# MLA attention heads 0 to 14: probability tiles turned by VectorE blocks and DRAM instead of TensorE

## The chip, the cores and the metric

One core of a Trainium2 chip. The metric is the device time of one execution in microseconds (us). Before the change it is 2168.78 us, the median of three runs (2168.34 to 2168.89).

## The reference

The program is two model blocks in one launch, for 512 tokens of width 1024 in float32. The first block is a gated mix of a convolution and a forgetting attention, then a feed-forward network. The second block puts 16 meta tokens in front (528 tokens), runs an RWKV-7 mixer and then an MLA (multi-head latent attention) mixer. The change touches only the MLA mixer, whose attention is this:

```python
for s, e in bounds:                       # blocks of 128 queries
    sc = (einsum('bqhd,bkhd->bhqk', q_nope[:, s:e], k_nope[:, :e])
          + einsum('bqhr,bkr->bhqk', q_rope[:, s:e], k_rope[:, :e])) * scale
    p = softmax(where(mask, sc, neg), axis=-1)
    outs.append(einsum('bhqk,bkhd->bqhd', p, v[:, :e]))
o = concatenate(outs, axis=1).reshape(B, L, D_INNER)
return (o * silu(g)) @ w_out
```

There are 16 heads. Each has 128 + 64 query and key features and 128 value features. A query block t (0 to 3) sees 16 + 128(t+1) keys.

## The kernel before

**Data.** Products in full precision are made from three float32r products (`product`, lines 161 to 163): high times high, low times high, high times low. Weights come from DRAM into one of two `raw` buffers, and POOL splits each into `w_hi` (L149) and `w_lo` (L152). Such a weight unit is either one head's `gate` (1024 columns) or a unit `A` or `B` (1280 columns) that holds what two heads need. `load_mla` issues the loads on SP; a load of unit u waits until unit u-1's count of splits shows that its buffer is free.

**One head.** `head_pe`, `head_act` and `head_dve` write out by hand what TensorE (PE), ScalarE (ACT) and VectorE (DVE) do for head h. On PE, before the change: scores of tiles 0 and 1 (L161 to L163, L2752, L2753); the first fills, which are `v0` and `v1` (the values of two heads) in an even head and `rope` (rotated queries of two heads) in an odd one; the value product of head h-1 (`values`, L2791 and L2793); the turns of tiles 0 and 1; scores of tile 2; in an even head `v2`; half of a gate fill; scores of tile 3; the fills `ka`, `qn`, `kb`, which are the next head's keys and queries; the other half of the gate; the turns of tiles 2 and 3.

**A tile's way.** Scores lie in PSUM banks 0 and 1. DVE adds the causal mask and takes the maximum (`maximum`, L2930, L2934). ACT takes the exponential and its sum (L2896). DVE takes the reciprocal (L2939) and, for tiles 2 and 3, scales the tile (L2944); for tiles 0 and 1 ACT does (L2902). The tile is 128 queries by keys, but the value product needs keys on the partitions: `turn` transposes it on PE in pieces of 128 columns into bank 2 or 3 (L2775), one more piece holding the 16 keys that lie beyond (L2777), and `turned_out` copies the result to `probT` (L2952, and L2951 for the 16 rows). `gated` multiplies the finished head by its gate and rounds it (L2919, L2921); POOL makes the low part (`z_low`, L2986).

**Banks and orders that matter.** `v0` and `v2` share bank 4: `v2` may start only when ACT has copied `v0` out (L2674), and that copy waits for `values` of the head before (`act.wait_ge(oo_mm, 2 * x)`), because it overwrites the buffer that `values` reads. `ka` and `kb` share bank 5: `kb` may start only when DVE has made the low part of `ka` (`low_out`, L2699), which stands behind `normalise(3)` in DVE's order. The first fill of a head needs the unit that POOL splits once `kb` of the head before is done. In POOL's order a head's gate split comes next, then `z_low`. `rope_parts` (L2723, a copy; L2725, a subtraction) stands behind the reciprocals of tiles 0 and 1 in even heads and behind `maximum(3)` in odd ones.

**SP.** Before the change SP issues all unit loads in order, then three rows of the output weights (`load_out_rows`). The load of the third waits until POOL has split the first, which waits for the last gate fill in head 14.

Of the kernel before, what the change touches and what calls it, by code (L numbers as in the profile page):

```python
# [70 lines left out]
def program(nc, io, out):  # L71
    with ExitStack() as base:
# [219 lines left out]
        x_land = [sem(f"x_land{t}") for t in range(QB)]  # L292
# [2142 lines left out]
        prob = xT[:, 5:7, :].rearrange("p a b -> p (a b)")  # L2435
        put = region(64)
# [322 lines left out]

        def turn_bank(t):  # L2760
            return 2 + t % 2

        def spill_cols(h, t):

            at = P * min(t + 1, QB - 1)
            return (turn_bank(t) if t < QB - 1 else value_bank(0) if h < MH - 1 else 2), at

        def turn(pe, h, t):
            pe.wait_ge(sc_norm, 4 * h + t + 1)
            if h or t >= 2:  # L2770
                pe.wait_ge(pt_ev, 4 * h + (0, 0, 1, 2 if h < MH - 1 else 3)[t])
            if h and t == QB - 1:
                pe.wait_ge(zt_ev, h)
            for c in range(t + 1):
                nc.tensor.transpose(ps[:, turn_bank(t), P * c:P * c + P], prob_cols(t, P * c, P), ident[:])  # L2775
            bank, at = spill_cols(h, t)
            nc.tensor.transpose(ps[:, bank, at:at + P], prob_cols(t, P * (t + 1), P), ident[:]).then_inc(pt_mm, 1)  # L2777
# [4 lines left out]
        def values(pe, h):  # L2782

            e, bank = h % 2, value_bank(h)
            pe.wait_ge(pt_ev, 4 * h + 4)
            pe.wait_ge(fill_act, ACT_AFTER[FILL_AT["v2", h // 2]])
            if h:
                pe.wait_ge(zt_ev, h)
            for c in range(QB):
                q = slice(max(P * c - N_META, 0), T1)  # L2790
                nc.tensor.matmul(ps[:, bank, q], v_tok[:, c, e, :], probT[:, c, q], start=(c == 0), stop=False)  # L2791
            q = slice(T1 - N_META, T1)
            nc.tensor.matmul(ps[:, bank, q], v_tok[:, QB, e, :], probT[:, QB, q], start=False, stop=True).then_inc(oo_mm, 1)  # L2793
# [31 lines left out]
        def head_pe(pe, h):  # L2825
# [12 lines left out]
            if h:  # L2838
                values(pe, h - 1)
            turn(pe, h, 0)  # L2840
            turn(pe, h, 1)
            scores(pe, h, 2)
            between(1)
# [9 lines left out]
            turn(pe, h, 2)  # L2853
            turn(pe, h, 3)
# [32 lines left out]
        def head_act(act, h):  # L2887
            slots = items_of(h)
            for t in range(QB):
                act.wait_ge(sc_max, 4 * h + t + 1)  # L2890
                if h or t >= 2:
                    act.wait_ge(pt_mm, 4 * h + max(t - 1, 0))
# [32 lines left out]
        def head_dve(dve, h):  # L2925
# [20 lines left out]
            def turned_out(t):  # L2946
                dve.wait_ge(pt_mm, 4 * h + t + 1)
                if h:
                    dve.wait_ge(oo_mm, h)
                bank, at = spill_cols(h, t)  # L2950
                nc.vector.tensor_copy(probT[0:N_META, t + 1, P * t + P - 32:P * t + P], ps[0:N_META, bank, at + P - 32:at + P])  # L2951
                nc.vector.tensor_copy(probT[:, 0:t + 1, P * t:P * t + P],  # L2952
                                      ps[:, turn_bank(t), 0:P * (t + 1)].rearrange("p (a b) -> p a b", b=P)).then_inc(pt_ev, 1)
            turns = h % 2 == 1 and h < MH - 1
# [6 lines left out]
            if h:  # L2961
                gated(dve, h - 1)
            turned_out(0)
            turned_out(1)
# [3 lines left out]
            normalise(2)  # L2968
            if h == MH - 2:
# [4 lines left out]
            normalise(3)  # L2974
            if h + 1 < MH:
# [4 lines left out]
            turned_out(2)  # L2980
            turned_out(3)
# [7 lines left out]
        with nc.Block() as block:  # L2989
            @block.sync  # L2990
            def _(sp):
# [21 lines left out]
                for unit in MLA_UNITS:  # L3013
                    load_mla(sp, unit)
                for k in range(2):
                    load_out_rows(sp, k)
                load_out_rows(sp, 2)
# [344 lines left out]
```

## Time and profile before

| what | us |
|---|---|
| median of three runs | 2168.78 |
| the profiled execution | 2170.27 |
| its span, first to last instruction | 2168.5 |
| the stretch of the 16 heads, first score matmul to last value matmul | about 1765 to 2083 |

The 16 heads take some 318 us of the span. One head takes about 20 us. The profile is of one execution; its times are microseconds from the span's start. A matmul's start is exact and its end modelled, so the distance between the starts of two matmuls is what the first one costs PE.

### The profile page before, as it was taken

How to read it: one execution, taken by the hardware profiler on the slowest of the kernel's cores; microseconds unless marked ns; L12 is line 12 of the kernel's file. 1: busy time of each engine (PE TensorE's matmuls, PEld its weight loads, DVE VectorE, ACT ScalarE, POOL GpSimd, SP SyncE). 2: the span in 40 equal slices, each digit the busy share in tenths (PEclk: the TensorE clock that was granted, in tenths of full speed). 3: DMA queues.
4: the chain of work that ended last, by engine and by line, in shares of the span. 5: the costliest groups of instructions: out<-in, count | busy, mean ns of one | idle time of the engine just before them, and what ended most of it. 6: DMA issues, size and time to landing. Idle time of an engine off the chain costs nothing.

```text
span 2168.5 us, 50089 instructions
## 1 busy us (share of the span) xinstructions
PE 2141.5 (99%) x20795; PEld 1715.8 (79%) x20795; DVE 1284.7 (59%) x2558; ACT 836.7 (39%) x1726; POOL 1175.3 (54%) x829
## 2 busy tenths in 40 slices
PE   8999999999999999999999999999999999999999
PEld 6888887788888767777777777777779788888877
DVE  5465467877850666666666666666652476656621
ACT  4122212333320354555555555555432444444410
POOL 5555566688766264544555544544566453443455
PEclk9999999999999999999999999999999999999999
DMA  4322323333332143333333333333534322222132
GB/s 131 88 78 78 88 88 91 94 97 97 97 110 96 42 126 87 83 82 83 82 92 83 88 87 91 88 90 92 145 79 126 107 78 54 67 56 54 54 129 95
DMA packets 368490, 193.77 MB, mean 89 GB/s; under 512 B 124411, under 2 KB 348793, under 8 KB 367881
## 3 DMA queue, kind: packets, MB, share of 16 engines
q1 hardware_dynamic: 368074, 190.50, 31.8%
q8 instruction: 166, 2.72, 0.5%
q14 instruction: 59, 0.48, 0.1%
q10 hardware_dynamic: 191, 0.07, 0.0%
HBM read 159.18 MB, written 18.52 MB: 82 GB/s over the span
## 4 chain that ended last, share of the span: by engine, by line
PE 93%; DVE 3%; POOL 1%; ACT 1%; issue 1%; DMA 0%; SPq 0%; DVEq 0%; POOLq 0%; ACTq 0%
PE ps L1452 21%; PE ps L161 16%; PE ps L162 15%; PE ps L163 15%; PE ps L1691 4%; PE ps L1707 3%; PE ps L1566 2%; PE ps L1737 2%; PE ps L1680 2%; PE ps L2791 2%; PE ps L1606 1%; PE ps L1651 1%; PE ps L1599 1%; PE ps L1638 1%; PE ps L2775 1%
## 5 line engine op out<-in xcount | busy, mean ns | idle before, releaser
L152 POOL TENSOR_TENSOR w_lo<-raw,w_hi 128x1024 fp32r<-128x1024 f32 (+1 forms) x163 | 416.1, 2553 | 13.6
L149 POOL TENSOR_SCALAR w_hi<-raw 128x1024 fp32r<-128x1024 f32 (+1 forms) x163 | 182.3, 1118 | 399.6 <-PE ps L163 383.2
L161 PE MATMUL ps<-h_hi,w_hi 128*128 128x512 f32 x616 | 242.9, 394 | 2.9 <-DVE h_lo L1129 1.7
L162 PE MATMUL ps<-h_lo,w_hi 128*128 128x512 f32 x616 | 240.8, 391 | 0.0
L163 PE MATMUL ps<-h_hi,w_lo 128*128 128x512 f32 x616 | 240.7, 391 | 0.0
L1452 PE MATMUL ps<-mixed_k,raw 128*64 128x264 f32 x1024 | 146.6, 387 | 0.0
L1452 PE MATMUL ps<-mixed_r,raw 128*64 128x264 f32 x1024 | 144.0, 387 | 0.2 <-ACT ws_b L1771 0.2
L161 PEld LDWEIGHTS ps<-h_hi,w_hi 128*128 128x128 f32 x616 | 116.1, 188 | 28.7 <-DVE h_lo L1129 2.6
L1452 PE MATMUL ps<-mixed_g,raw 128*64 128x264 f32 x1024 | 137.6, 387 | 0.0
L163 PEld LDWEIGHTS ps<-h_hi,w_lo 128*128 128x128 f32 x616 | 116.1, 189 | 24.4
L162 PEld LDWEIGHTS ps<-h_lo,w_hi 128*128 128x128 f32 x616 | 116.2, 189 | 23.1
L1144 DVE SCALAR_TENSOR_TENSOR up_c<-up_raw,params,up_c 128x512 f32<-128x512 f32 x88 | 114.5, 1304 | 22.6 <-ACT up_c L862 21.1
L1452 PE MATMUL ps<-mixed_v,raw 128*64 128x264 f32 x1024 | 125.4, 388 | 0.0
L2083 DVE TENSOR_TENSOR x_m<-ps,lv_pad 128x640 f32<-128x640 f32 (+2 forms) x160 | 110.9, 726 | 16.4 <-PE ps L1691 11.8
L1691 PEld LDWEIGHTS ps<-t_m,mb 128*64 128x64 f32 x2752 | 96.7, 138 | 15.4 <-DVE t_m L2089 0.4
L1691 PE MATMUL ps<-t_m,mb 128*64 128x64 f32 x2752 | 96.9, 222 | 0.2 <-DVE t_m L2089 0.2
L1452 PEld LDWEIGHTS ps<-mixed_v,raw 128*64 128x64 f32 x1024 | 71.2, 137 | 31.3
L2896 ACT ACTIVATE xT<-ps,nmax 128x144 f32<-128x144 f32 (+1 forms) x64 | 34.6, 541 | 135.6 <-DVE nmax L2934 135.3
L1707 PEld LDWEIGHTS ps<-x_m,t_t 128*64 128x64 f32 x2240 | 77.1, 138 | 10.5 <-DVE x_m L2083 0.6
L2026 DVE COPY uv<-ps 64x64 f32<-64x64 f32 x160 | 34.8, 217 | 85.3 <-PE ps L1638 84.8
L2032 DVE TENSOR_SCALAR uv<-ps,ec_c 64x64 f32<-64x64 f32 x144 | 39.9, 277 | 68.2 <-PE ps L1651 67.7
L855 ACT ACTIVATE up_raw<-ps 128x512 f32<-128x512 f32 x40 | 24.0, 599 | 145.3 <-PE ps L163 145.3
(499 smaller groups left out, 5793.4 us busy)
## 6 DMA issues: line engine op xcount, KB each, us to landing
raw<-in_rwkv_w_in_dram SPq DMA_DIRECT2D x64, 512.0 KB, 4.4
raw<-in_w_up_dram SPq DMA_DIRECT2D x44, 512.0 KB, 3.9
raw<-in_w_in_dram SPq DMA_DIRECT2D x41, 512.0 KB, 3.9
raw<-in_w_down_dram SPq DMA_DIRECT2D x22, 512.0 KB, 3.5
raw<-in_mla_w_in_dram SPq DMA_DIRECT2D x22, 512.0 KB, 4.0
sb_kept<-xT SPq DMA_DIRECT2D x16, 528.0 KB, 2.6
xT<-sb_kept SPq DMA_DIRECT2D x16, 528.0 KB, 3.8
raw<-in_mla_w_out_dram SPq DMA_DIRECT2D x16, 512.0 KB, 3.6
```

What stands on the lines that cost most here:

```text
L149: nc.gpsimd.tensor_scalar(w_hi[s][:, 0:width], raw[s][:, 0:width], 1.0, 0.0, ALU.mult, ALU.add).then_inc(split_hi, 1)
L152: nc.gpsimd.tensor_tensor(w_lo[s][:, 0:width], raw[s][:, 0:width], w_hi[s][:, 0:width].bitcast(F32), ALU.subtract).then_inc(split_ready, 1)
L161: nc.tensor.matmul(dst, w[0], x[0], start=start, stop=False)
L162: nc.tensor.matmul(dst, w[0], x[1], start=False, stop=False)
L163: return nc.tensor.matmul(dst, w[1], x[0], start=False, stop=stop)
L1144: nc.vector.scalar_tensor_tensor(out=up_c[:, ab, 1 + k, :], in0=up_raw[:, n % 4, 1 - k:1 - k + T1], scalar=prm(("cf1", "cf0")[k], n // 2 + ...
L1452: mm = nc.tensor.matmul(dst[m, :], raw_k[t % 2][:, k, m], mixed[t][:, k, cols], start=(k == 0), stop=(k == KD - 1))
L1566: mm = nc.tensor.matmul(ps[r, banks[h], 0:T2 // 2], WHOLE_W[n][:, P * b + r.start:P * b + r.stop], z_whole[:, k, at:at + T2 // 2], start=s ...
L1680: mm = nc.tensor.matmul(ps[:, 2 + 3 * h + q, x * P:x * P + P], bk[own[h], c0 + x, :], rkv[own[h], c0 + x, 0:2 * C], start=True, stop=True)
L1691: mm = nc.tensor.matmul(ps[own[h], 2 + p, x * C:x * C + C], mb[:, c0 + x, own[h]], t_m[:, c0 + x, :], start=True, stop=True)
L1707: mm = nc.tensor.matmul(dst, t_t[:, c0 + x, :], x_m[:, c0 + x, h, :], start=True, stop=True)
L2083: nc.vector.tensor_tensor(x_m[:, c0:c0 + m, :, :], part_of(2 + p, m).unsqueeze(2).to_broadcast([P, m, 2, C]), lv_pad[:, lv - 1, :, :].unsq ...
```

## The change

In heads 0 to 14 PE turns nothing. DVE transposes each tile in blocks of 32 by 32 (`blocked`), in SBUF; that leaves each block turned in its own place. SP then writes the tile to DRAM with four DMAs, one for each 32 partitions (`write_blocks`), whose runs of 32 elements land so that the DRAM tensor holds the tile with keys as rows, and reads it back into `probT` with one DMA (`read_turned`). The piece with the 16 last keys is turned by a second small DVE transpose and copied (`spilled`). Head 15 keeps the turns on PE. `values` of a head stands one place later in the next head, behind the scores of tile 2. `gated` stands behind `blocked(2)` instead of ahead of `maximum(2)`. The loads of weights are interleaved with the DMAs of the heads: six units ahead of them, then one behind the writes of tiles 0 and 1 and one behind the last reads of each head. Two DRAM scratch tensors per tile alternate from head to head. The core of the diff:

```diff
@@ -2433,6 +2433,11 @@
         assert put.end <= 121
         probT, z_t = xT[:, 0:5, 0:T1], xT[:, 7, 0:T1]
         prob = xT[:, 5:7, :].rearrange("p a b -> p (a b)")
+        p_last = region(154)("p_last", [P, T1 + 32])
+        p_scr = [[nc.dram_tensor(f"p_scr{t}_{e}", [P * (t + 1), P], F32, kind="Internal").ap() for t in range(QB)] for e in range(2)]
+        p_blocked, p_written, p_here = x_land[0:3]
+        LANDED0 = 16
+        BLOCKED, WRITTEN, HERE = 4, 256, 64
         put = region(64)
         o_tok = put("o_tok", [P, QB, D])
         squares = put("squares", [P, QB, D])
@@ -2757,19 +2762,64 @@
             slot = T2 * (1 - t % 2)
             return prob[:, slot + at:slot + at + n]
 
+        def blocks_of(t):
+
+            return (wa_in[:, 0:P], wa_in[:, P:3 * P], wa_in[:, 0:3 * P], p_last[:, 0:T1])[t]
+
+        def spill_of(t):
+
+            return wa_in[0:32, 3 * P + 32 * t:3 * P + 32 * t + 32]
+
+        def write_blocks(sp, h, t):
+            sp.wait_ge(p_blocked, LANDED0 + BLOCKED * h + t + 1)
+            if t == 0 and h > 1:
+                ge(sp, p_here, LANDED0 + HERE * (h - 1))
+            for a in range(4):
+                sp.dma_start(p_scr[h % 2][t].rearrange("(b i) q -> i b q", i=32)[:, :, 32 * a:32 * a + 32],
+                             blocks_of(t)[32 * a:32 * a + 32, :].rearrange("i (b j) -> i b j", j=32)).then_inc(p_written, 16)
+
+        def read_turned(sp, h, t):
+            q = slice(P * t, P * t + P)
+            sp.dma_start(probT[:, 0:t + 1, q], p_scr[h % 2][t].rearrange("(c p) q -> p c q", p=P)).then_inc(p_here, 16)
+
+        def turned_by_dma(sp, h, loads):
+
+            written = LANDED0 + WRITTEN * h
+            write_blocks(sp, h, 0)
+            write_blocks(sp, h, 1)
+            next(loads, None)
+            sp.wait_ge(p_written, written + 128)
+            ge(sp, oo_mm, h)
+            read_turned(sp, h, 0)
+            read_turned(sp, h, 1)
+            write_blocks(sp, h, 2)
+            write_blocks(sp, h, 3)
+            sp.wait_ge(p_written, written + WRITTEN)
+            read_turned(sp, h, 3)
+            read_turned(sp, h, 2)
+            next(loads, None)
+
+        def unit_loads(sp):
+            for unit in MLA_UNITS:
+                load_mla(sp, unit)
+                yield
+            for k in range(3):
+                load_out_rows(sp, k)
+                yield
+
         def turn_bank(t):
             return 2 + t % 2
 
         def spill_cols(h, t):
 
             at = P * min(t + 1, QB - 1)
-            return (turn_bank(t) if t < QB - 1 else value_bank(0) if h < MH - 1 else 2), at
+            return (turn_bank(t) if t < QB - 1 else 2), at
 
         def turn(pe, h, t):
             pe.wait_ge(sc_norm, 4 * h + t + 1)
-            if h or t >= 2:
-                pe.wait_ge(pt_ev, 4 * h + (0, 0, 1, 2 if h < MH - 1 else 3)[t])
-            if h and t == QB - 1:
+            if t >= 2:
+                pe.wait_ge(pt_ev, 4 * h + (1, 3)[t - 2])
+            if t == QB - 1:
                 pe.wait_ge(zt_ev, h)
             for c in range(t + 1):
                 nc.tensor.transpose(ps[:, turn_bank(t), P * c:P * c + P], prob_cols(t, P * c, P), ident[:])
@@ -2782,6 +2832,8 @@
         def values(pe, h):
 
             e, bank = h % 2, value_bank(h)
+            if h < MH - 1:
+                pe.wait_ge(p_here, LANDED0 + HERE * (h + 1))
             pe.wait_ge(pt_ev, 4 * h + 4)
             pe.wait_ge(fill_act, ACT_AFTER[FILL_AT["v2", h // 2]])
             if h:
@@ -2835,11 +2887,13 @@
             scores(pe, h, 1)
             between(0)
             first_out(pe, h, 0)
-            if h:
+            if h == MH - 1:
                 values(pe, h - 1)
-            turn(pe, h, 0)
-            turn(pe, h, 1)
+                turn(pe, h, 0)
+                turn(pe, h, 1)
             scores(pe, h, 2)
+            if 0 < h < MH - 1:
+                values(pe, h - 1)
             between(1)
             if h == MH - 2:
                 fill(pe, FILL_AT["gate", MH - 1], range(5, KD))
@@ -2850,8 +2904,9 @@
             if h + AHEAD < MH:
                 fill(pe, FILL_AT["gate", h + AHEAD], range(2, 5) if h == MH - 3 else range(4, KD))
             first_out(pe, h, 3)
-            turn(pe, h, 2)
-            turn(pe, h, 3)
+            if h == MH - 1:
+                turn(pe, h, 2)
+                turn(pe, h, 3)
 
         def out_pe(pe):
 
@@ -2888,8 +2943,10 @@
             slots = items_of(h)
             for t in range(QB):
                 act.wait_ge(sc_max, 4 * h + t + 1)
-                if h or t >= 2:
-                    act.wait_ge(pt_mm, 4 * h + max(t - 1, 0))
+                if h == MH - 1 and t >= 2:
+                    act.wait_ge(pt_mm, t - 1)
+                elif h or t >= 2:
+                    act.wait_ge(p_blocked, LANDED0 + BLOCKED * h + max(t - 1, 0))
                 dst = prob_cols(t, 0, keys(t))
                 if t == QB - 1:
                     dst = dst.rearrange("p (a b) -> p a b", a=2)
@@ -2944,41 +3001,67 @@
                 nc.vector.tensor_scalar(p, p, prec[:, t % 2:t % 2 + 1], None, ALU.mult).then_inc(sc_norm, 1)
 
             def turned_out(t):
-                dve.wait_ge(pt_mm, 4 * h + t + 1)
-                if h:
-                    dve.wait_ge(oo_mm, h)
+                dve.wait_ge(pt_mm, t + 1)
+                dve.wait_ge(oo_mm, h)
                 bank, at = spill_cols(h, t)
                 nc.vector.tensor_copy(probT[0:N_META, t + 1, P * t + P - 32:P * t + P], ps[0:N_META, bank, at + P - 32:at + P])
                 nc.vector.tensor_copy(probT[:, 0:t + 1, P * t:P * t + P],
                                       ps[:, turn_bank(t), 0:P * (t + 1)].rearrange("p (a b) -> p a b", b=P)).then_inc(pt_ev, 1)
-            turns = h % 2 == 1 and h < MH - 1
+
+            def blocked(t):
+                dve.wait_ge(sc_norm, 4 * h + t + 1)
+                if t == 0:
+                    ge(dve, p_written, LANDED0 + WRITTEN * h)
+                    ge(dve, pt_ev, 4 * h)
+                elif t == 2:
+                    dve.wait_ge(p_written, LANDED0 + WRITTEN * h + 128)
+                nc.vector.transpose(blocks_of(t), prob_cols(t, 0, P * (t + 1)))
+                slot = T2 * (1 - t % 2) + P * (t + 1)
+                nc.vector.transpose(spill_of(t), prob[96:P, slot:slot + 32]).then_inc(p_blocked, 1)
+
+            def spilled(t):
+                dve.wait_ge(p_blocked, LANDED0 + BLOCKED * h + t + 1)
+                ge(dve, oo_mm, h)
+                nc.vector.tensor_copy(probT[0:N_META, t + 1, P * t + P - 32:P * t + P], spill_of(t)[0:N_META, :]).then_inc(pt_ev, 1)
+            last = h == MH - 1
+            turns = h % 2 == 1 and not last
             maximum(0)
             maximum(1)
             normalise(0)
             normalise(1)
             if not turns and h < MH - 1:
                 rope_parts(dve, h + 1)
-            if h:
+            if last:
                 gated(dve, h - 1)
-            turned_out(0)
-            turned_out(1)
+            for t in range(2):
+                turned_out(t) if last else blocked(t)
             maximum(2)
             if turns:
                 rope_turned(dve, h // 2 + 1)
             normalise(2)
+            if not last:
+                blocked(2)
+                if h:
+                    gated(dve, h - 1)
+                for t in range(3):
+                    spilled(t)
             if h == MH - 2:
                 gate_out(dve, MH - 1)
             maximum(3)
             if turns:
                 rope_parts(dve, h + 1)
             normalise(3)
+            if not last:
+                blocked(3)
+                spilled(3)
             if h + 1 < MH:
                 for kind in ("ka", "qn", "kb"):
                     low_out(dve, (kind, h + 1))
             if h + AHEAD < MH - 1:
                 gate_out(dve, h + AHEAD)
-            turned_out(2)
-            turned_out(3)
+            if last:
+                turned_out(2)
+                turned_out(3)
 
         def z_low(pool, h):
             pool.wait_ge(zt_ev, h + 1)
@@ -3010,11 +3093,13 @@
                 sp.dma_start(h_rows_kept, h_rows[:]).then_inc(s_h, 16)
                 for n in range(4, 7):
                     load_in(sp, n)
-                for unit in MLA_UNITS:
-                    load_mla(sp, unit)
-                for k in range(2):
-                    load_out_rows(sp, k)
-                load_out_rows(sp, 2)
+                loads = unit_loads(sp)
+                for _ in itertools.islice(loads, 6):
+                    pass
+                for h in range(MH - 1):
+                    turned_by_dma(sp, h, loads)
+                for _ in loads:
+                    pass
                 sp.wait_ge(unit_done, UNIT_AT["gate", MH - 1] + 1)
                 sp.wait_ge(s_h, 48)
                 sp.dma_start(h_fin[:], h_rows_kept).then_inc(s_h, 16)
```

## Rows read from the trace of the kernel before

**Rows 1.** Windows, the heads: length, busy time of engines, clock, DMA share, GB/s.

```profile
1785.00:2046.00 261.00, 259.99 (x1505) 221.18 (x1505) 158.42 (x407) 125.25 (x254) 113.96 (x65) 1.00 0.23 60
```

**Rows 2.** Timeline of PE, heads 6 and 7: start, duration, what.

```profile
1884.85 0.31 PE L161 MATMUL ps<-kn_hi,qn_hi 128*128 128x144 f32 x1
...
1891.32 0.31 PE L2775 MATMUL ps<-ident,xT 128*128 128x128 f32 x1
...
1891.82 0.43 PE L161 MATMUL ps<-kn_hi,qn_hi 128*128 128x400 f32 x1
...
1892.81 0.28 PE L161 MATMUL ps<-w_hi,ckv_hi 128*16 128x256 f32 x1
...
1901.59 0.29 PE L163 MATMUL ps<-ckv_hi,w_lo 128*128 128x264 f32 x1
...
1904.51 0.49 PE L2775 MATMUL ps<-ident,xT 128*128 128x128 f32 x3
...
1905.40 0.31 PE L161 MATMUL ps<-kn_hi,qn_hi 128*128 128x144 f32 x1
...
1906.68 0.40 PE L161 MATMUL ps<-cq_hi,w_hi 128*128 128x512 f32 x1
...
1920.91 0.36 PE L161 MATMUL ps<-ckv_hi,w_hi 128*128 128x264 f32 x1
...
1925.40 0.31 PE L161 MATMUL ps<-kn_hi,qn_hi 128*128 128x144 f32 x1
```

**Rows 3.** Timeline of POOL, around heads 6 and 7.

```profile
1887.28 2.39 POOL L152 TENSOR_TENSOR w_lo<-raw,w_hi 128x1024 fp32r<-128x1024 f32 x1
...
1902.19 1.26 POOL L149 TENSOR_SCALAR w_hi<-raw 128x1280 fp32r<-128x1280 f32 x1 [8.07 <-PE ps L163]
1903.54 2.94 POOL L152 TENSOR_TENSOR w_lo<-raw,w_hi 128x1280 fp32r<-128x1280 f32 x1
```

**Rows 4.** Timeline of ACT, head 6.

```profile
1891.57 1.09 ACT L2674 ACTIVATE v_tok<-ps 128x512 f32<-128x512 f32 x2 [0.94 <-PE ps L2793]
```

**Rows 5.** Timeline of DVE, heads 6 and 7.

```profile
1888.16 1.79 DVE L2723 CAST qr<-q_rot 64x512 fp32r<-64x512 f32 x1
...
1900.22 0.43 DVE L2699 TENSOR_TENSOR kn_lo<-ps,kn_hi 128x264 fp32r<-128x264 f32 x1
...
1911.98 0.69 DVE L2919 TENSOR_TENSOR xT<-ps,gate 128x512 f32<-128x512 f32 x1 [3.30 <-PE ps L2793]
...
1914.92 0.69 DVE L2708 SCALAR_TENSOR_TENSOR q_rot<-ps,cos_t 128x512 f32<-128x512 f32 x1 [0.25 <-ACT q_sw L2660]
...
1917.50 0.30 DVE L2930 TENSOR_TENSOR ps<-ps,causal 128x128 f32<-128x128 f32 x1
...
1920.22 0.43 DVE L2699 TENSOR_TENSOR kn_lo<-ps,kn_hi 128x264 fp32r<-128x264 f32 x1
```

**Rows 6.** Groups of DVE by shape: busy, mean ns of one, idle before.

```profile
L2092 DVE STREAM_TRANSPOSE t_t<-t_m 128x320 f32<-128x320 f32 x64 | 32.7, 512 | 2.2
L2008 DVE STREAM_TRANSPOSE e_both<-bk 128x128 f32<-128x128 f32 x120 | 31.7, 285 | 4.6 <-POOL bk L2151 4.6
```

**Rows 7.** Timeline of SP, one burst of small copies in the RWKV stage.

```profile
1209.35 12.21 SPq L2315 DMA_DIRECT2D bk_rows<-e_both  x16
```

**Rows 8.** One line of the kernel, these copies: count, ns min/median/max, first and last.

```profile
L2315 SPq DMA_DIRECT2D bk_rows<-e_both x240: 595/611/1767, 800.0 to 1527.6; - x120
```

**Rows 9.** DMA, that burst's stretch 1209:1222: packets, MB, share; KB, landing.

```profile
q1 hardware_dynamic: 5195, 1.05, 40.9%
...
bk_rows<-e_both SPq DMA_DIRECT2D x16, 32.0 KB, 2.5
```

**Rows 10.** DMA, the heads 1790:2070: packets, MB, share; KB, landing.

```profile
q1 hardware_dynamic: 32210, 17.80, 22.9%
...
raw<-in_mla_w_q_up_dram SPq DMA_DIRECT2D x12, 256.0 KB, 3.3
```

**Rows 11.** Timeline of SP, heads 14 and 15.

```profile
2048.09 13.95 SPq L136 DMA_DIRECT2D raw<-in_mla_w_out_dram  x2
```

More of the change, by code:

```diff
@@ L290, in program @@
         x_copied = sem("x_copied")
-        x_land = [sem(f"x_land{t}") for t in range(QB)]
+        x_land = [sem(n) for n in ("x_land0_p_blocked", "x_land1_p_written", "x_land2_p_here", "x_land3")]
         low = region(0)
```

## Prediction

> **What bounds the kernel now.** I read four views. First the busy times by stage: over the heads PE is busy 260.0 of 261 us at full clock, DVE 158 us, and the DMA engines 23% [rows 1]. So a head lasts as long as PE's list of work, and PE's work taken away is a gain only if nothing else that PE waits for is as late. Second, PE's timeline of an even and the next odd head: head 6 starts at 1884.85, head 7 at 1905.40, head 8 at 1925.40, so 20.55 and 20.00 us; I write "place" for the time since a head's first score matmul [rows 2]. Third, what stands beside PE on the other engines at the places the change touches [rows 3 to 5]. The reader is to see there that three waits of PE are met with hardly anything to spare:
> - *The split.* POOL ends `w_lo` at 1903.54 + 2.94 = 1906.48, and PE starts `rope`, which needs it, at 1906.68 [rows 2, 3]. Where PE does wait, a start follows a release by about that. Between the end of `kb` (1901.59 + 0.13 = 1901.72) and that start PE has 4.96 us of other work, all of it needed as cover.
> - *The copy of v0.* In even heads ACT copies `v0` out only after the value product (1891.57) [rows 4]; PE has 1.49 us between the end of that product (1891.32) and `v2` (1892.81) [rows 2], in which the copy fits.
> - *The low part of ka.* In an odd head DVE ends it at 1920.65 and PE starts `kb` at 1920.91 [rows 2, 5]; PE's own work would let it start 0.2 us sooner. DVE already decides there. In the even head the same part ends at 1900.65 and `kb` starts at 1900.97: 0.3 us to spare at most.
>
> Fourth, SP and the DMA views, for what the new copies cost [rows 7 to 11].
>
> **What is removed.** Turns of tiles 0 and 1: 1891.32 to 1891.82, 0.50 us. Of tiles 2 and 3: 1904.51 to 1905.40, 0.89 us [rows 2]. 1.4 us a head, 15 heads: 21 us of PE. The DVE copies from PSUM go too.
>
> **What is added, engine by engine.**
>
> *DVE.* A block transpose of 128 columns takes 285 ns, of 320 columns 512 ns [rows 6], 1.2 ns a column, so about 0.44, 0.57 and 0.71 us for 256, 384 and 512. They take the place of PSUM copies of nearly the same cost, and four small transposes come on top (the same line gives 0.17 us at 32 columns). The sum matters little; the order does. Before, `gated` and the copies of tiles 0 and 1 ran from 1911.98 to the mask of tile 2, while DVE had time. Now `blocked(2)` (0.65), `gated` (1.07) and three `spilled` (0.3) stand between `normalise(2)` and `maximum(3)`, and `blocked(3)` and `spilled(3)` (0.9) ahead of the low part of `ka`: 2.9 us more on the chain to `kb`.
>
> Odd head, place by place. The rotation of the queries waits for ACT's copies as before (1914.92 is place 9.5) [rows 5]; with `normalise(2)` it ends at 12.0, `blocked(2)` at 12.7, `gated` at 13.7, `spilled` at 14.0. From the mask of tile 3 to `ka`'s low part takes 1920.22 - 1917.50 = 2.7 us with the rope parts [rows 5], to 16.8; plus 0.9, and 0.43 for itself: 18.2; `kb` at 18.45. PE gets there at 15.7 (15.5 before, less the 0.5 of the turns, plus 0.85 of the next part, less the 0.2 it already waited). Wait 2.7, of which 0.2 was there: +2.5 us.
>
> *POOL.* The turns of tiles 2 and 3 were cover for the split. PE's work there falls from 4.96 to 4.07 and its start does not: +0.85 us in each of 14 heads.
>
> *ACT.* `v2` now follows the value product directly. Release 0.25, copy 0.6, release 0.2: 1.05 us of waiting in each even head from 2 on. (In head 0 the cover shrinks as well; about 1 us.)
>
> *SP and DMA.* No row shows a store to DRAM of runs of 128 bytes. The nearest is the RWKV stage's copy of 32 KB pieces, also runs of 128 bytes: 16 issues in 12.21 us, 0.76 us each [rows 7], 2.5 us from issue to landing [rows 9]. In that stretch a packet took 0.409 x 16 x 13 / 5195 = 16 ns; in the heads, with runs of 512 bytes and 256 bytes, 0.229 x 16 x 280 / 32210 = 32 ns [rows 9, 10]. A head's 5120 small packets over 16 engines are then 5 to 10 us of a head's time on top of 23%: not a bound. The issues are: sixteen stores are 12.2 us of SP, four reads and two units' loads 4.2 us more. I take 0.76 and 2.5 us, as the burst has the same run, partitions and destination stride; the ends are 0.61, an issue's own time [rows 8], and 2.0 below, and 0.76 and 4 above. A read of up to 256 KB lands in 3.3 us [rows 10].
>
> In an odd head the stores of tiles 0 and 1 start at 3.9 and are landed at 11.8, ahead of `blocked(2)`, which waits for them since the buffer is shared. In an even head they start later. `rope_parts` stands ahead of `blocked(0)`, and its copy ended at 1889.95 after 1.79 us, when POOL's `w_lo` had ended at 1889.67 [rows 3, 5]; it takes 0.4 us otherwise. POOL's gate split now ends at place 5.7 (it starts when the wait for the split ends), so `blocked(0)` ends at 7.05, eight issues start by 12.4 and the last is landed at 14.9. `blocked(2)` comes at 15.0 instead of 12.4, and `kb` at 21.2 where PE is ready at 17.5: a wait of 3.7 us.
>
> The Trainium skill has a rule for that copy (SBUF — State Buffer, Who interferes with whom): a copy in VectorE's two-port mode and a GpSimd instruction exclude each other for the whole instruction, and an operation with two SBUF inputs is also kept out by one that reads SBUF. By it the subtraction behind the copy waits too; without it, `blocked(0)` would come 2 us sooner and the even head's wait would fall to 1.3 us, 17 us less in all.
>
> The end of the DMA chain itself is covered: in an odd head `blocked(3)` ends at 17.6, its stores are landed at 22.4, reads issued at 22.5 and 23.0 land by 26.2; `values` is due at 22.0 + 5.9 = 27.9. In an even head: 20.4, 25.2, 29.0, due at 24.7 + 5.9 = 30.6.
>
> *The end.* The load of the third output row now stands in SP's order of head 14 behind the stores of tiles 0 and 1, ahead of everything else of that head. It waits for POOL's split of the first row; before, it was the second load of a pair that took 13.95 us in all, to 2062.0 [rows 11], place 15.7 of head 14. `z_low(13)` stands ahead of that split and follows `gated`, now at place 17 or later, so the load goes at 22.5. Behind it the reads, eight stores (6.1 us) and two reads end at place 35.4 of head 14. Head 15 wants `values(14)` at place 2, that is 26.7. PE waits 8.9 us, once.
>
> **The sum.** An odd head: 20.0 - 1.4 + 0.85 + 2.5 = 22.0, +2.0. An even head: 20.55 - 1.4 + 0.85 + 1.05 + 3.7 = 24.7, +4.2. Seven odd heads +13.7; heads 2 to 12, +25; head 0 +2 (its stores start earlier); head 14 +5.5 (`kb` waits longest there, as fewer gate products stand ahead of it); the end +8.9. Together +55 us. The profiled execution took 2170.3 us, 1.5 more than the median, which I subtract: 2168.8 + 55 = 2224.
>
> **Rivals.**
>
> *The copies are cheap, only the orders on DVE, ACT and POOL cost.* With issues of 0.6 us and landings of 2.0, and `blocked(0)` not held by POOL, `blocked(2)` is never late: even heads 22.1, odd 22.0, the end 7: +28 to +32, 2199. For it: an issue's own time is 0.61 us [rows 8]. Against: the held copy of 1.79 us.
>
> *Stores to DRAM are slow.* If they land in 4 us and reads in 4, both kinds of heads become a chain of stores, reads and `values`: 24.2 and 26.2 us, +85, 2254; at 5 us, +108. For it: nothing in the rows stores such runs. Against: 16 to 32 ns a packet. The Trainium skill speaks for it (DMA: Bandwidth & Descriptors, Specifications): transfers under 512 bytes are done as read-modify-write. No run here shows it yet.
>
> *The `spilled` copies are held by `z_low`.* They read and write SBUF, as the held copy does, and POOL's 1.3 us `z_low` starts with them. Up to 1.1 us a head on the chain to `kb`: +15 on the forecast, 2239. The page cited on shared ports would have it so; but the first of the three starts before POOL does.
>
> *Faster: the waits hide in each other.* PE loses 21 us of work, and the one wait that certainly comes is the split's, 14 x 0.85 = 12. If DVE reaches `ka`'s low part before PE wants `kb` (place 15.7 in an odd head), and the stores land, the kernel is 9 us faster, 2160. That needs DVE 2.5 us quicker than the rows have it; the point that decides is whether `maximum(3)` starts by place 11.8.
>
> **How the numbers follow.** Forecast 0.45; cheap copies 0.22; slow stores 0.14; held `spilled` 0.10; faster 0.06; a balance within 0.2% 0.03. The predicted time is the forecast's, 2224. From 2190 to 2260 takes in the cheap copies, the held ones and most of the slow stores, and leaves out some 0.2. A measurement of this kernel tells 0.2% (4.3 us) from no change. Faster 0.06, same 0.03, slower 0.91.
>
> **What would show it.** In the profile after: heads of about 22 and 24.7 us in turn; PE waits at L161 for POOL's `w_lo`, for ACT's copy of `v0` in even heads and, longest, for DVE's `kn_lo`; DVE's tile 2 transpose in even heads released by a DMA; one wait of 9 us for the reads ahead of the last `values`. Wrong would be: heads of one length (the stores never hold `blocked(2)`), waits of PE for `probT`'s reads in every head (slow stores), or no wait for `kn_lo` (faster).

## The result: 2.4% slower, and the profile after

The changed kernel takes 2220.8 us (median of 4 runs, 2218.7 to 2223.4) against 2168.8 before: ratio 1.0238, 95% interval 1.0220 to 1.0256. The prediction was 2224. The profiled execution has a span of 2217.0 us, before 2168.5: 48.5 us more. Of these 41.8 lie between the first scores of head 0 and of head 15 (341.7 us, before 299.9), 5.7 behind (109.2 us, before 103.5) and 1.0 ahead.

First the window that answers [rows 1], with the busy time of PE first and that of DVE third: PE fell from 260.0 to 226.3 us busy of 261, DVE stayed as it was (158 us), the DMA share doubled to 0.49, and the mean clock is no longer 1.00.

```profile
1785.00:2046.00 261.00, 226.28 (x1187) 188.57 (x1186) 158.16 (x401) 109.07 (x224) 106.11 (x59) 0.96 0.49 110
```

Second, what PE waited for in 1764 to 2140, and DVE for a DMA (total us, times, longest):

```profile
PE ps L161 <- DVE kn_lo L2704: 37.7, 15, 3.8
...
PE ps L161 <- ACT v_tok L2679: 6.3, 8, 0.8
...
PE ps L161 <- POOL w_lo L152: 5.0, 8, 0.7
...
DVE wa_in L3018 <- DMA p_scr<-wa_in: 4.0, 3, 2.0
...
PE ps L2843 <- DMA xT<-p_scr: 2.6, 1, 2.6
```

PE's four waits and DVE's one are the predicted ones, at other sizes. Third, PE's timeline of head 7 (start 1924.88) and head 8 (1948.67), which answers to [rows 2]:

```profile
1924.88 0.23 PE L161 MATMUL ps<-kn_hi,qn_hi 128*128 128x144 f32 x1
...
1943.60 0.56 PE L161 MATMUL ps<-ckv_hi,w_hi 128*128 128x264 f32 x1 [2.86 <-DVE kn_lo L2704]
...
1945.06 0.63 PE L161 MATMUL ps<-u_hi,w_hi 128*128 128x512 f32 x1
1945.48 0.63 PE L162 MATMUL ps<-u_lo,w_hi 128*128 128x512 f32 x1
...
1948.67 0.23 PE L161 MATMUL ps<-kn_hi,qn_hi 128*128 128x144 f32 x1
...
1957.11 0.28 PE L161 MATMUL ps<-w_hi,ckv_hi 128*16 128x256 f32 x1 [0.84 <-ACT v_tok L2679]
...
1968.29 0.36 PE L161 MATMUL ps<-ckv_hi,w_hi 128*128 128x264 f32 x1 [2.84 <-DVE kn_lo L2704]
```

Read the starts behind 1943.60. Two matmuls of 512 columns start 0.42 us apart; in the kernel before they stood 0.23 apart. From `kb` to the next head are 5.07 us; where the clock stayed up they are 3.60, behind the equally long wait at 1968.29 too (next head at 1971.89). The windows show the granted clock (the figure behind the five busy times) at 1.00 in the wait, half of full, the lower level of 1.2 GHz, behind it, and back at 2.4 GHz some 3 us later:

```profile
1941.00:1943.00 2.00, 0.00 (x0) 0.00 (x0) 1.85 (x7) 0.45 (x1) 0.00 (x0) 1.00 0.00 0
1943.00:1945.00 2.00, 1.40 (x6) 1.43 (x7) 0.94 (x3) 0.00 (x0) 0.00 (x0) 0.61 0.53 81
1945.00:1947.00 2.00, 2.00 (x7) 1.61 (x6) 0.43 (x1) 0.39 (x1) 1.34 (x2) 0.53 0.33 50
1947.00:1949.00 2.00, 2.00 (x12) 1.64 (x11) 0.13 (x1) 0.00 (x0) 2.00 (x1) 1.00 0.75 225
```

This happens in heads 0, 1, 5, 7, 9, 11 and 13, and once more from the end of head 14 (behind a wait of 3.26 us) into head 15. No step of the prediction had it. Last, VectorE in head 8, with the rope copy that POOL held and the stretch between `normalise(2)` and `ka`'s low part, and the stores and reads of one head (SP's timeline; the DMA view of 1785:2083):

```profile
1951.68 2.21 DVE L2728 CAST qr<-q_rot 64x512 fp32r<-64x512 f32 x1
...
1961.80 0.58 DVE L3018 STREAM_TRANSPOSE wa_in<-xT 128x384 f32<-128x384 f32 x1 [1.69 <-DMA p_scr<-wa_in]
...
1962.63 0.69 DVE L2976 TENSOR_TENSOR xT<-ps,gate 128x512 f32<-128x512 f32 x1
...
1963.95 0.28 DVE L2987 TENSOR_TENSOR ps<-ps,causal 128x128 f32<-128x128 f32 x1
...
1966.56 0.71 DVE L3018 STREAM_TRANSPOSE p_last<-xT 128x512 f32<-128x512 f32 x1
...
1967.62 0.41 DVE L2704 TENSOR_TENSOR kn_lo<-ps,kn_hi 128x264 fp32r<-128x264 f32 x1
```
```profile
1928.92 4.58 SPq L2778 DMA_DIRECT2D p_scr<-wa_in  x8
...
1942.83 1.93 SPq L2778 DMA_DIRECT2D p_scr<-p_last  x4
1946.25 0.93 SPq L2783 DMA_DIRECT2D xT<-p_scr  x2
```
```profile
q1 hardware_dynamic: 120622, 32.41, 48.1%
...
p_scr<-p_last SPq DMA_DIRECT2D x52, 64.0 KB, 2.0
...
p_scr<-wa_in SPq DMA_DIRECT2D x52, 32.0 KB, 1.7
```

A store takes SP 0.57 us on the mean of these eight (4.58 / 8) and 0.48 of these four (1.93 / 4), not the 0.76 of [rows 7]. The eight hold one slow store of 1.20 us; the median of all 240 stores is 0.45, and the slowest took 1.84. By size, the median landing is 1.7 to 2.2 us, not 2.5 [rows 9].

### The profile page after: what moved, and what is told of

Read it like the earlier page. It is cut to its first block, busy times and chain, and to the rows that moved or that the text cites. A ratio compares the mean times of both kernels' runs of the same rounds, so it can differ in the third digit from the quotient of the medians.

```text
span 2217.0 us, 50040 instructions
## 1 busy us (share of the span) xinstructions
PE 2140.9 (97%) x20585; PEld 1707.1 (77%) x20585; DVE 1309.9 (59%) x2618; ACT 836.4 (38%) x1726; POOL 1176.7 (53%) x829
## 4 chain that ended last, share of the span: by engine, by line
PE 83%; DVE 8%; issue 3%; ACT 3%; POOL 1%; SPq 1%; DMA 1%; DVEq 0%; POOLq 0%; ACTq 0%
PE ps L1452 21%; PE ps L161 14%; PE ps L162 13%; PE ps L163 13%; PE ps L1691 3%; PE ps L1707 3%; PE ps L1566 2%; PE ps L1737 2%; PE ps L1680 2%; PE ps L1606 1%; PE ps L1651 1%; DVE nmax L2991 1%; PE ps L1599 1%; SPq L2778 1%; PE ps L1638 1%
## 5 line engine op out<-in xcount | busy, mean ns | idle before, releaser
L163 PEld LDWEIGHTS ps<-h_hi,w_lo 128*128 128x128 f32 x616 | 116.5, 189 | 24.8
L162 PEld LDWEIGHTS ps<-h_lo,w_hi 128*128 128x128 f32 x616 | 116.7, 189 | 23.2
L2083 DVE TENSOR_TENSOR x_m<-ps,lv_pad 128x640 f32<-128x640 f32 (+2 forms) x160 | 110.9, 726 | 16.4 <-PE ps L1691 11.8
L3069 POOL TENSOR_TENSOR z_lo<-xT,z_hi 128x512 fp32r<-128x512 f32 x16 | 20.7, 1292 | 141.5 <-DVE z_hi L2978 141.5
L161 PE MATMUL ps<-u_hi,w_hi 128*128 128x512 f32 (+1 forms) x200 | 80.4, 402 | 0.0
```

The costliest lines, as they stand in the source:

```text
L161: nc.tensor.matmul(dst, w[0], x[0], start=start, stop=False)
L162: nc.tensor.matmul(dst, w[0], x[1], start=False, stop=False)
L163: return nc.tensor.matmul(dst, w[1], x[0], start=False, stop=stop)
L2083: nc.vector.tensor_tensor(x_m[:, c0:c0 + m, :, :], part_of(2 + p, m).unsqueeze(2).to_broadcast([P, m, 2, C]), lv_pad[:, lv - 1, :, :].unsq ...
```

## The experiments

All are edits of the changed kernel, except the last but one. Times are medians; the ratio is to the kernel before, run beside them (2168.6 to 2170.7 us). "How much less" is counted from the changed kernel's 2220.8 us unless another run is named.

**`ka`'s low part first.**

```diff
+                low_out(dve, ("ka", h + 1))
                 blocked(3)
                 spilled(3)
             if h + 1 < MH:
-                for kind in ("ka", "qn", "kb"):
+                for kind in ("qn", "kb"):
```

> VectorE takes ka's low part directly after the normalisation of tile 3, ahead of tile 3's blocks and spill. Theory (VectorE's order holds ka's bank, and with it kb's product): in head 7 the ka subtraction starts 1.05 us sooner (1941.88 instead of 1942.93), so kb's wait falls from 2.84 to 1.8 us in the odd heads and from 1.2 to about 0.2 in the even ones: 15 x 1.05 = 16 us, and some 10 us more if TensorE's granted clock no longer falls after the shorter wait: 2195 to 2205 us. Tile 3's blocks start 0.7 us later, which costs at most 0.7 us at head 14. Rival (the copies through DRAM or a later wait set the head): the time stays at 2215 to 2221 and the wait turns up before the values or before the scores.

2196.0 us, ratio 1.0129 (1.0114 to 1.0144): 24.8 us less than the change. The waits for `kn_lo` halve, and 3.60 us from `kb` to the next head is now the rule; of heads 0 to 12 only head 5, with 2.70 us of wait, kept a long one (4.89). The price is at the end: head 14's values waited 4.5 us for their reads (2.6 in the changed kernel), where 0.7 us more had been expected at most.

```profile
PE ps L161 <- DVE kn_lo L2704: 18.6, 10, 2.7
...
PE ps L161 <- POOL w_lo L152: 9.6, 14, 1.3
```

One instruction moved past three gives back half of the loss, part of it by the clock. VectorE's order sets how long `kb` waits; the next run shows that it waits at all because it shares a bank with `ka`.

**`kb` in a bank of its own** (`"kb": 5` becomes `"kb": 2`).

> kb's product gets a PSUM bank of its own (bank 2, which no turn uses now in heads 0 to 14); VectorE's order is untouched. Theory: the 37.7 us of kb waits go, POOL's split of the next weights starts as much sooner and its 9.5 us of waits go too, and the clock stays up (some 10 us); what is left is a wait of up to 0.7 us ahead of the next head's scores in the odd heads, since kb's own low part still ends behind ka's: about 2168 us, 2160 to 2180. Rival (VectorE as a whole, not the shared bank, sets the head): the wait only moves to the next head's first scores, 2205 to 2220.

2185.7 us, 1.0078 (1.0061 to 1.0095): 35 us less, not 53. The wait for `kn_lo` ahead of `kb` is gone, and eleven of the heads 0 to 12 last 18.1 to 20.9 us. But heads 5, 6, 13 and 14 last 22.8, 21.6, 21.9 and 21.5 us. There the rival is right: PE waited 3.38, 3.87 and 1.77 us for `kn_lo` at the start of heads 6, 14 and 15 instead. In the heads before these POOL ran beside VectorE's scaling of tile 3, which took 1.18, 1.29 and 2.64 us instead of 0.49; the later runs take this up. The tail stayed 8 us longer than before.

**No DMAs for the turned tiles** (stores, reads and their waits left out).

> All stores to and reads from the two DRAM buffers are left out, with their waits (most of each turned tile is then stale, so the output is not the reference's); VectorE's blocks and spills stay. Theory (VectorE's order is the cost, the copies are covered): only the three waits of tile 2's blocks for stores (4.0 us), the wait of head 14's values (2.6 and 3.3 us) and a little more go: 2205 to 2213. Rival (the traffic itself is the cost, by held buffers, late weights or shared ports): below 2190.

2206.0 us, 1.0169 (1.0153 to 1.0184): 15 us less, as the theory had it; most of the turned tiles are stale there. `kb`'s waits are unchanged, 2.81 to 2.84 us in six of seven odd heads and 1.20 in even ones, and the clock still falls in heads 1, 7, 9, 11 and 13. The copies through DRAM are not what costs most.

```profile
1936.47 0.36 PE L161 MATMUL ps<-ckv_hi,w_hi 128*128 128x264 f32 x1 [2.84 <-DVE kn_lo L2704]
```

**No large block transposes** (`blocks_of` transposed in head 0 only).

> The four large block transposes of heads 1 to 14 are left out (their DMAs, the 32 x 32 spills and every wait stay; the output is not the reference's). Theory: VectorE has 2.05 us less a head, of which 0.58 and 0.71 (tiles 2 and 3) lie ahead of ka's low part in any case: 14 x 1.3 = 18 us, some 10 us more by the clock: 2190 to 2203. If the copies through DRAM set the head: within 6 us of 2221, since the stores would start less than 1 us sooner.

2197.1 us, 1.0130 (1.0115 to 1.0145). `kb`'s wait is 1.52 to 1.54 us in most odd heads and 0.21 in most even ones: 1.3 and 1.0 us less, with all DMAs in place. That the DMAs set the length of a head falls with this run and the last.

```profile
1932.75 0.36 PE L161 MATMUL ps<-ckv_hi,w_hi 128*128 128x264 f32 x1 [1.54 <-DVE kn_lo L2704]
```

**The third output row behind head 14's reads** (`next(loads)` behind `write_blocks(sp, h, 1)` only for `h < MH - 2`).

> Only SP's order in head 14 differs from the changed kernel: the third row of the output weights, whose load waits for POOL's split of the first, is loaded behind the reads of head 14's turned tiles. Theory (that wait delays the reads and the values of head 14): the values' wait of 2.6 us in head 15 and the slow clock behind it (4.12 us for eight matmuls in place of 2.40) go: 3 to 5 us less, 2216 to 2218; the last stretch from head 15's start to the end falls from 109.2 us towards the 103.5 of before. Rival (POOL's late split and not the reads hold the end): the wait moves to the output's first cells and the time stays within 1 us.

2217.3 us, 1.0211 (1.0198 to 1.0225): 3.5 us less, though its interval overlaps that of the change. The trace is clearer: the wait for the reads falls from 2.58 to 0.41 us, and the tail from 109.2 to 107.7. The clock was still low (8 matmuls of the values in 3.57 us, not 2.40), and scores(3) waited 1.26 us. The expectation had put the low clock down to the values' wait. It had fallen before that: in the changed kernel the window 2108 to 2112, ahead of that wait, has a granted clock of 0.50, behind the 3.26 us that head 14's `kb` waited (3.22 in this run).

**TensorE kept busy in the wait.**

```diff
+            if kind == "kb" and x > 0 and (x == 1 or x % 2 == 0):
+                for _ in range(10):
+                    nc.tensor.matmul(ps[:, 3, :], cq_hi[:, 0, 0:P], cq_hi[:, 0, :], start=True, stop=True)
```

> Ten matmuls of 512 columns, whose result nobody reads, are put ahead of kb's product in head 0 and the odd heads (2.3 us at full clock, inside a wait of 2.8 us or more), in bank 3. Theory (TensorE's fall to half clock behind the wait costs 1.5 us in seven heads, kb's start to the next head's start 5.07 us instead of 3.60): all intervals come to 3.6 us; 7 x 1.47 = 10 us less, of which 0.67 us a head comes back as a wait for POOL's split (6 x 0.67 = 4): about 2215 us. Rival (the interval is long for another reason, or the clock falls anyway): 2219 to 2224 and intervals of 5.07 us still there.

2214.4 us, 1.0206 (1.0193 to 1.0219): 6.4 us less with 80 matmuls more, whose result nobody reads. The interval from `kb` to the next head is 3.58 to 3.61 us in heads 0 to 12, the mean clock of 1785:2046 is 1.00, and POOL's wait of 0.67 us is back in all of heads 1 to 13. Timeline of head 7 there:

```profile
1941.30 0.36 PE L161 MATMUL ps<-ckv_hi,w_hi 128*128 128x264 f32 x1 [0.58 <-DVE kn_lo L2707]
...
1944.90 0.23 PE L161 MATMUL ps<-kn_hi,qn_hi 128*128 128x144 f32 x1
```

**`gated` and the first three spills behind `maximum(3)`.**

> Only VectorE's order differs from the changed kernel: gated(h-1) and the spills of tiles 0 to 2 stand behind maximum(3) instead of ahead of it. Theory (VectorE's order ahead of maximum(3) delays exp(3) and by it kb): in head 7 scores(3) ended at 1937.3 and the mask of tile 3 started at 1938.83, so exp(3) comes 1.3 to 1.4 us sooner, the 1.4 us now lie partly beside exp(3) (VectorE idle 0.86 us there), and kb's wait falls by 0.9 to 1.1 us in even heads and by little more than 0.3 in odd ones, where the copies only change places with rope's parts: 8 to 12 us less and a few for the clock: 2205 to 2213. Rival (POOL's low part of z, which starts when gated is done, holds normalise(3), which needs VectorE's fast mode): kb's waits grow by 1 us in some heads, and the time is 2218 to 2235.

2240.2 us, 1.0322 (1.0306 to 1.0337): slower by 19 us, the rival's case. The theory that everything ahead of `maximum(3)` should go behind it falls. In even heads the mask of tile 3 now follows scores(3) at once, but POOL's low part of z starts with `normalise(3)`, and that takes 1.40 instead of 0.49 us in seven heads; in five of seven odd ones (1, 3, 7, 9 and 11) the second of the rope parts takes 1.64 instead of 0.69, and in the other two the third spill copy takes 1.25 instead of 0.16.

```profile
1928.27 1.39 DVE L3001 TENSOR_SCALAR xT<-xT,prec 128x528 f32<-128x528 f32 x1
```
```profile
1928.09 1.29 POOL L3070 TENSOR_TENSOR z_lo<-xT,z_hi 128x512 fp32r<-128x512 f32 x1 [11.51 <-DVE z_hi L2978]
```

VectorE's instruction ends (1929.66) some 0.3 us after POOL's (1929.38).

**Two banks and the end's order** (`kb` in bank 2, `v2` in bank 3).

> The changed kernel with kb's product in bank 2, v2's in bank 3 (both free in heads 0 to 14) and the third output row's load behind head 14's reads. Expected from the run with kb's bank alone (2185.7 us): the waits of v2 for the copy of v0 (0.84 us in seven even heads, 0.4 in head 0) go, 6.3 us, and 3 to 5 us at the end: 2175, 2171 to 2180. Rival (the 0.84 us is a wait for v0's copy that qn, in the same bank, then meets): 2182. Heads of 19.2 to 19.8 us against 20.0 and 20.5 of the kernel before.

2183.6 us, 1.0062 (1.0046 to 1.0077), where 2171 to 2180 was expected. The waits for `v0`'s copy are gone, so even heads are 0.7 us shorter (19.9); but heads 5, 8, 9 and 13 last 24.0, 23.1, 21.9 and 21.9 us. There POOL's split started ahead of `normalise(3)`, or in head 8 0.04 us behind, and held it. Head 14 (22.9 us) shows the same, 2.61 us for the scaling; it and heads 6 and 10 (21.6 and 21.0) also start at the lower clock, behind waits of 4.04, 4.87 and 3.36 us. DVE and POOL in head 5:

```profile
1881.63 2.82 DVE L3002 TENSOR_SCALAR xT<-xT,prec 128x528 f32<-128x528 f32 x1
1884.48 0.71 DVE L3019 STREAM_TRANSPOSE p_last<-xT 128x512 f32<-128x512 f32 x1
```
```profile
1879.60 1.27 POOL L149 TENSOR_SCALAR w_hi<-raw 128x1280 fp32r<-128x1280 f32 x1 [1.33 <-PE ps L163]
1880.94 3.21 POOL L152 TENSOR_TENSOR w_lo<-raw,w_hi 128x1280 fp32r<-128x1280 f32 x1
```

In head 7 `normalise(3)` started at 1925.12, POOL at 1925.19, and it took 0.50 us. So some tenths of a microsecond decide over 2 to 4. Part of the gain from an earlier `kb` is given back because it starts POOL earlier.

**All low parts first, one gate block later in the head** (besides the two banks).

> As the kernel with both banks and the end's order, and besides: VectorE takes all three low parts ahead of tile 3's blocks and spill, and one block of each gate product moves from the slot ahead of scores(3) to the end of the head, so that 0.7 us more work stands between kb's product and the product that waits for POOL's split. Theory: the waits for POOL (0.67 us in odd, 0.26 in even heads) and the late low parts of heads 5, 13 and 14 (3.4, 3.9 and 1.8 us) go: 15 us less than its sister: 2162, 2157 to 2170, faster than the kernel before (2168.6). Rival (tile 3's turned copy, now 1.7 us later, becomes what the values wait for, or scores(3) waits for the exponential): heads of 20 us and a time above 2172.

2206.1 us, 1.0166 (1.0153 to 1.0179), 22 us slower than its sister: a miss, and the rival's case. POOL's wait did go in heads 1 to 13, but tile 3's blocks come 1.7 us later, and now the values wait for the reads in every head, some 2.1 us in even ones:

```profile
PE ps L2844 <- DMA xT<-p_scr: 25.3, 15, 5.5
```

The chain of copies was covered in the changed kernel, but a shift of 1.7 us, in shorter heads, uncovers it.

**ScalarE normalises tile 3 and copies the spills; head 14's values behind scores(2)** (besides the two banks).

> From the run with two banks (2183.6 us), with ScalarE in place of VectorE for tile 3's normalisation and the four spill copies (both were held by POOL's split in heads 5, 8, 9 and 13: 2.82 us instead of 0.49, 1.80 instead of 0.17), and with head 14's values and the turns of tiles 0 and 1 of head 15 behind scores(2). Theory (the long heads of that run come from VectorE's instructions that POOL holds): all heads 1 to 13 come to 19.2 to 19.9 us, 16 us less; the values of head 14 no longer wait 2.2 us with a slow clock behind: 3 to 4 us less: 2164, 2158 to 2170, against 2168.6 to 2170.7 of the kernel before. Rival (the long heads come from something else, such as late stores): heads of 22 to 24 us remain and the time is 2175 or more.

2167.6 us, ratio 0.9989 (0.9980 to 0.9998): as fast as the kernel before, or up to 0.2% faster. Heads 1 to 13 last 19.6 to 19.8 us but for two (20.7, 20.1), as the theory had it: the long heads came from VectorE's instructions that POOL held. The run by itself doesn't separate this from a second effect, since it also takes some 1.2 us of work a head off VectorE (0.49 + 4 x 0.17); that the held instructions are the cause rests on their durations in the run with two banks. ScalarE's own are not held. These are groups of ACT by shape in 1785:2060; the scaling took 736 to 740 ns each time, though POOL was running during part of it in most heads:

```profile
L2945 ACT ACTIVATE xT<-wa_in 16x32 f32<-16x32 f32 x55 | 10.8, 220 | 29.0 <-DVE wa_in L3034 29.0
...
L2978 ACT ACTIVATE xT<-xT,prec 128x528 f32<-128x528 f32 x14 | 10.3, 738 | 4.4 <-DVE prec L3010 4.4
```

All 15 take 294.8 us against 299.9; the tail, from head 15's start to the end, takes 106.3 against 103.5. The gain in the heads is therefore 5.1 us, and 2.8 of it are lost behind them.

**The kernel before with fewer turns** (the ten column transposes of heads 0 to 14 left out).

> The kernel before, without the ten column transposes of each of the heads 0 to 14 (the four that turn the last block and signal stay, and VectorE's copies too; the turned tiles are then stale and the output is not the reference's). It measures the gain term alone. Theory: ten transposes at 0.108 us are 1.08 us a head, 16 us in 15 heads; seven of them (0.76 us) stood between kb's product and the product that waits for POOL's split, where the changed kernel shows 0.67 us of wait after losing 0.87, so about 0.56 us comes back in 13 heads, 7 us: 2160 us, 2157 to 2163. Rival (no wait behind it): 2153. Rival (VectorE or ScalarE bound the head already): 2167 to 2170.

2167.1 us, 0.9989 (0.9981 to 0.9998): 3 us for 16 us of work, where the theory had 10. Two starts of PE in that run:

```profile
1918.06 0.36 PE L161 MATMUL ps<-ckv_hi,w_hi 128*128 128x264 f32 x1 [0.20 <-DVE kn_lo L2699]
...
1923.68 0.39 PE L161 MATMUL ps<-w_hi,ckv_hi 128*128 128x256 f32 x1 [0.46 <-POOL w_lo L152]
```

The 0.76 us ahead of a head come back as 0.61 (scores to first fill 1.89 us, before 1.28) and 0.11 behind it; in odd heads the 0.32 ahead of scores(2) come back as 0.25 ahead of `kb`, in even ones they are kept. A wait listed as 0.46 costs 0.6 to 0.7, as the first matmul behind it takes 0.23 us to the start of the next and not 0.12.

**The first output cells later** (as the version with ScalarE's spills).

> As the version with ScalarE's spills (2167.55 us), but the first cell of the output product, which stood at the end of head 14 and waited 1.76 us for POOL's split of the output weights, is put into head 15, and the cell (1, 1, 1) ahead of head 15's turns of tiles 2 and 3, where TensorE waited 1.68 us for a normalised tile. Theory: the first wait goes and 0.7 us of the second is filled: 2.4 us less, 2165 us, 2163 to 2168. Rival (POOL's split of the second row is then late instead): 2167 to 2168.

2167.6 us, 0.9991 (0.9982 to 1.0000): nothing gained. The wait for POOL's `w_lo` in head 14 gave way to one of 3.67 us for `kn_lo` at the start of head 15.

## Why the prediction was right, and where it was not

The waits were the right ones, and the way and size of the whole came out. That the sum (+55) and the result (+52) are so close is luck, as large errors cancel. Stretch by stretch, in us, measured between the two profiled executions:

| stretch | forecast | measured |
|---|---|---|
| seven odd heads | +13.7 | +27.3 |
| heads 2 to 12, even | +25 | +8.5 |
| head 0 | +2 | +3.6 |
| head 14 | +5.5 | +2.5 |
| from head 15 on | +8.9 | +5.7 |
| ahead of the heads, where nothing was changed | 0 | +1.0 |

The prediction wanted odd heads of 22 us and even ones of 24.7. It is the other way round: the odd heads last 22.3 to 24.9 us, the even ones from 2 to 12 last 21.4 to 23.2.

- *Turns removed, -21.* Of PE's work, right: the interval ahead of the next head lost 0.87 us (forecast 0.89). The run with fewer turns shows what 16 of these 21 us were worth by themselves: 3 us, as waits for POOL's split and, in odd heads, for `kn_lo` stood right behind.
- *POOL's split, 0.85 us in 14 heads, 11.9.* The size is right (0.67 us listed, some 0.8 in pace), the number is not: seven heads (3, 4, 5, 7, 9, 11, 13), about 5.5 us. In the others the slow clock or a longer wait at the end of the head before had given POOL its time.
- *The copy of v0, 1.05 us in even heads, 7.4.* Measured 0.84 in seven, 6.3 in all. Right.
- *VectorE's order.* Odd heads: a wait of 2.7 us was forecast, 2.83 to 2.86 stand in four of seven and 3.5 to 3.8 in three. Right, and shown by moving `ka`'s part and by leaving the blocks out. The longer three: in head 1 PE was ready sooner, as it had not waited for POOL; in head 5 a spill copy was held; in head 13 fewer gate products stand ahead of `kb`.
- *Even heads, +3.7.* This step failed. It put the issues at 0.76 us each, a landing at 2.5, and the end of POOL's gate split at place 5.7. POOL did hold the rope parts as assumed (the copy took 1.5 to 2.3 us in heads 2, 6, 8, 10 and 12, the subtraction 2.77 in heads 0 and 4). But its split ended at place 4.2 to 5.0 in all even heads from 2 to 12 except head 4, and eight stores took 3.7 us in head 6 and 5.3 in head 8, where one of them alone took 1.82. So `blocked(2)` waited for stores in heads 0, 2 and 8 only (4.0 us in all), and even heads waited 1.2 to 1.4 us ahead of `kb`, head 8 2.84. That is the 1.3 us of the rival of cheap copies, and its issues and landings (0.6 and 2.0 us) were near; its other condition, that POOL doesn't hold `blocked(0)`, was not met. Ahead of `kb` the six even heads cost 9.1 us instead of 22.
- *Head 14, +5.5.* `kb` waited 3.26 us there, less than in heads 1, 5 and 13, and the head grew by 2.5. In it POOL's split of the first output row held `normalise(3)` for 2.62 us instead of 0.49, which the prediction didn't have.
- *The clock.* Not in the prediction. Kept high, the seven intervals would have been 1.4 to 1.6 us shorter, in head 13 2.4 (5.30 against 2.89): 11.2 us gross; 6.4 us in time when it was taken away, since POOL's wait then returns. In the sum it fills most of the hole that the even heads left.
- *The end, +8.9.* The load of the third row was issued at 2103.79 and the reads behind it at 2104.24, as described, yet the values waited 2.58 us, as stores and landings were faster than assumed; at the slow clock they then took 4.12 us in place of 2.40. The same slow clock, from head 14's end, let PE reach the values 3.84 us behind the head's start, before 1.96. The tail is 5.7 us longer. The described wait is there, at 2.6 us instead of 8.9; the slow clock takes 1.9 and 1.7 us more.

For the heads: 36.3 (`kb`: 37.7 less the 0.2 us that each odd head lost before) + 11.2 (clock) + 6.3 (`v2`) + 5.5 (POOL) - 21 = 38 of the 41.8 us measured; where the other 3.5 lie is not shown.

Of the rivals, slow stores are refuted. The Trainium skill (DMA: Bandwidth & Descriptors, Specifications) would have them as read-modify-write below 512 bytes; here 0.481 x 16 x 298 / 120622 = 19 ns a packet over all copies and median landings of 1.7 to 2.2 us show no such price. Set against the run without these DMAs, the stores and read backs alone come to (0.483 - 0.203) x 16 x 261 / (106103 - 31680) = 16 ns a packet, an estimate from the two runs' windows 1785:2046. Of the held spills there was one (three of them took 1.57 us in head 5, 0.33 in the other heads), but the same holding set the later versions. The faster kernel needed `maximum(3)` by place 11.8; in head 7 it starts at 13.95.

## What to carry to other kernels

Work taken off the bounding engine is also cover for the others: before counting it as a gain, list what that engine needs right behind the place, and how late each of those is. If a wait of some 3 us appears on TensorE, add what the lower clock behind it costs. When VectorE has copies or scalings within SBUF next to POOL's long instructions, an earlier start of POOL can cost more than it brings; moving them to ScalarE removed most of that here.

## What the runs showed of the hardware

- In the changed kernel TensorE's granted clock went from 2.4 to 1.2 GHz behind waits of 2.8 to 3.8 us, but not behind each one: those of 2.84 us in heads 3 and 8 left it up. With `gated` behind, heads with a wait of 2.19 us show both, 5.14 us from `kb` to the next head in head 8 and 3.58 in head 10. With `ka`'s part first it stayed up behind waits of 1.7 to 1.8 us and one of 2.62 (head 13), and fell behind one of 2.70 (head 5).
- POOL's splits and low parts held VectorE's scaling within SBUF (0.49 became 1.18 to 2.82 us), its 16 x 32 copy (0.17 became 1.80) and a subtraction of two SBUF operands (0.69 became 1.80 in the two-bank run, 2.77 in the changed kernel), until about POOL's own end. Block transposes were not held: one started beside a running `w_lo` took its usual 0.71 us (1947.14 in the two-bank run, `w_lo` from 1946.91 to 1949.88), and ten of the fifteen of 512 columns in that run lie wholly inside a POOL instruction, at 0.71 us each. The Trainium skill (SBUF — State Buffer, Who interferes with whom) has this rule for the copies, the scaling and the subtraction, and the trace agrees.
- ScalarE's scaling of 128 x 528 took 736 to 740 ns in 15 of 15 (version with ScalarE's spills), with POOL running during part of 10 of them.
- Block transposes of 128, 256, 384 and 512 columns took 0.31, 0.45, 0.58 and 0.71 us, one of 32 x 32 0.20.
